# Index units ahead of the convolution units in a two-layer hybrid decoder step, with the index dots inside the convolution units

## The chip, the cores and the metric

The kernel runs on one core of one Trainium2 chip. The metric is the device time of one execution in microseconds (us). All times below are of the kernel before the change unless something else is said.

## The reference, cut to what matters

Two layers, each with one combined input projection, three parallel branches, and one output projection with a residual add. There are 528 prompt tokens (16 learned ones and 512) and 8 sample tokens; the model width is 1024.

```python
z = einsum('btd,dn->btn', rms_norm(x), w_in)            # 3624 columns
q, k, v, ga, qi, wi, ki, ub, gb, cv, cg, gc = split(z)
q = rope(rms_norm(q)); k = rope(rms_norm(k)); qi = rope(qi); ki = rope(ki)
uc = cv * sigmoid(cg)
# A: 8 index heads of 32 dims pick the keys of every query
sc = sum_h wi[h] * relu(qi[h] . ki * 32**-0.5) * 8**-0.5     # causal
idx = top_k(sc);  att = softmax attention over the picked keys
# B: causal pooling of ub.   C: depthwise convolution of width 31 over uc, LayerNorm, swish
y = concat(att * silu(ga), pool * silu(gb), conv * silu(gc)) @ w_out;  x = x + y
```

## The kernel before, in words

**Layout.** The prompt is cut into five token tiles of 16 (with the 8 sample tokens: 24 rows), 128, 128, 128 and 128 rows. The input projection is done in float32r, with the activations and the weights each split into a high part and a rest: three matmuls for every 128 rows of the contraction, so 24 for a unit. Names of engines: PE is the matmul engine, DVE the vector engine, ACT the scalar engine, POOL is GpSimd, SP issues the DMAs.

**Units.** A unit is one PSUM bank full of the projection. `unit_fm` (L1254) makes 128 channels by 268 tokens (half of them); `unit_tm` (L1236) makes one token tile by all columns of a group. The order of units (L124 to L127) is: eight convolution units `("conv", m, h)`, of which m = 0, 1 are the value channels (group cv) and m = 2, 3 the gate channels (group cg); five index units (296 columns: index queries, head weights, index key); five key units, five query units, five value units (512 columns each); then the units of `PLAN`, which lie between the 40 attention items (tile, head), and the output units. Each unit waits until the unit that had its bank before is evacuated (`open_unit`, L1215).

**Weights.** They come in pieces (`LOADS`, L69) into six slots by `m % 6`. SP loads a piece when the last unit that reads the slot is done (`w_load`, L624). ACT makes the high part (`high`, L942) and DVE the rest (`rest`, L1618); for the pieces of `REST_ON_POOL` (L84: two of q, two of v, and all from ub on) ACT scales and POOL makes the rest. `AHEAD` is the number of pieces of the first group (2 of four 128-row blocks). They are split at the very start in layer 0, and for layer 1 in step 41 and 42 of the items of layer 0 (`split_high` L377, `split_rest` L382).

**Start of layer 0.** SP issues the loads of x tiles 0 to 2, the two weight pieces, x tiles 3 and 4, constants, page table. SP then waits for the table and reads 16 page numbers (L620) before it issues anything else.

**Index.** ACT evacuates an index unit (`idx_evac`), POOL rotates it, PE transposes it (L1333), ACT keeps it in `qkT`. Then come 40 *pieces* (L141) of index scores: PE multiplies (`dots`, L1351, two pieces in a call, into bank 0 and 1 of A), ACT takes the relu in place (`relu`, L1038), DVE multiplies by the head weight and adds into `bias` (`gather`, L1671). `dots(first)` waits until DVE has gathered all earlier pieces. The 40 pieces lie in the key and query units: two behind each half of a unit.

**Keys and queries.** For every tile of k (numbers 0 to 4) and q (5 to 9): ACT copies the unit to `kz` (three buffers) and its square to `ksq` (`kq_evac`, L1014), DVE sums the squares (`kq_sum`, L1657), and POOL does all the rest in one chain (`kq_tile`, L858): power -0.5, two products over 512 columns, four operations of the rotation. POOL also makes the rests of four weight pieces between the tiles (L877). PE transposes the finished tile (`kq_turn`, L1341): tile n behind unit n+2, so that the last two (8 and 9) stand behind value units 0 and 1. `kq_evac(n)` waits for the transpose of tile n-3.

**DVE in between.** The convolution is 31 taps of two instructions each (`tap`, L1731) that accumulate in bank 2 and 3 of A: 8 taps beside the index units, 15 in the key units, 8 in the query units. Top-k is rounds of max and match_replace on `bias` (`select`, L1693); 20 of these steps lie in the query units (`between`, L1743), the others in a loop behind the query units (L1820) and in the attention items (`late`, L1719). PE's first attention scores of a tile are followed by DVE's `ttr` (L1969), which is queued behind that loop.

## Time and profile before

| what | value |
|---|---|
| time, median of 3 runs | 752.42 us (747.38, 752.42, 752.99) |
| profiled execution | 746.28 us, of which the span of the engines is 745.0 us |
| granted PE clock, mean over the span | 0.984 of full speed |
| PE (matmul) busy | 702.3 us, 94% of the span |
| DVE busy | 523.2 us, 70% |
| ACT busy | 331.2 us, 44% |
| POOL busy | 300.3 us, 40% |
| DMA | 71.90 MB, mean 97 GB/s |

The profile is of one execution. A line such as `L1260` is a line of the kernel. Matmuls overlap in their pipeline, so the busy time of PE is an upper bound of what it needs; the distance between starts is the better measure. A line `[1.20 <-DVE small L1969]` behind an instruction means that its engine was idle for 1.20 us before it and that a DVE instruction of line 1969 ended that idle time. Index dots appear as two records each, since they are float32.

### The profile page before, as it was taken

How to read it: one execution, taken by the hardware profiler on the slowest of the kernel's cores; microseconds unless marked ns; L12 is line 12 of the kernel's file. 1: busy time of each engine (PE TensorE's matmuls, PEld its weight loads, DVE VectorE, ACT ScalarE, POOL GpSimd, SP SyncE). 2: the span in 40 equal slices, each digit the busy share in tenths (PEclk: the TensorE clock that was granted, in tenths of full speed). 3: DMA queues.
4: the chain of work that ended last, by engine and by line, in shares of the span. 5: the costliest groups of instructions: out<-in, count | busy, mean ns of one | idle time of the engine just before them, and what ended most of it. 6: DMA issues, size and time to landing. Idle time of an engine off the chain costs nothing.

```text
span 745.0 us, 13366 instructions
## 1 busy us (share of the span) xinstructions
PE 702.3 (94%) x4690; PEld 567.3 (76%) x4690; DVE 523.2 (70%) x1320; ACT 331.2 (44%) x850; POOL 300.3 (40%) x445
## 2 busy tenths in 40 slices
PE   5899999999889999998999999999988799999998
PEld 5897756578777777776999866666878688777797
DVE  3538888899977977435663898989997777822232
ACT  5525646533947333334132555543485643332212
POOL 1013698942848710011120459895376763000000
PEclk9999999999989999999999999999999899999999
DMA  5543040314232536014025304031522244501203
GB/s 195 160 137 118 17 128 30 114 35 143 58 87 60 179 136 227 1 58 139 21 92 153 126 4 142 30 88 46 157 58 61 83 151 167 170 1 57 96 22 112
DMA packets 54979, 71.90 MB, mean 97 GB/s; under 512 B 12977, under 2 KB 30585, under 8 KB 54881
## 3 DMA queue, kind: packets, MB, share of 16 engines
q1 hardware_dynamic: 54802, 70.96, 30.0%
q8 instruction: 38, 0.62, 0.4%
q14 instruction: 28, 0.23, 0.1%
q10 hardware_dynamic: 111, 0.08, 0.0%
HBM read 64.05 MB, written 7.61 MB: 96 GB/s over the span
## 4 chain that ended last, share of the span: by engine, by line
PE 70%; DVE 21%; ACT 3%; issue 2%; DMA 2%; POOL 1%; SPq 0%; ACTq 0%; DVEq 0%; POOLq 0%
PE R L1273 16%; PE R L1260 6%; PE R L1244 6%; PE R L1262 6%; PE R L1261 6%; PE R L1245 6%; PE R L1246 6%; DVE bias L1715 5%; DVE small L1713 5%; PE R L1409 4%; PE A L1360 3%; PE A L1213 2%; PE A L1438 2%; DVE W_r L1614 2%; PE R L1213 1%
## 5 line engine op out<-in xcount | busy, mean ns | idle before, releaser
L1260 PE MATMUL R<-x_hi,W_r 128*128 128x268 f32 x448 | 137.7, 307 | 5.9 <-DVE bufA L1614 3.3
L1262 PE MATMUL R<-x_hi,W_r 128*128 128x268 f32 x448 | 133.3, 297 | 0.0
L1261 PE MATMUL R<-x_lo,W_r 128*128 128x268 f32 x448 | 133.0, 297 | 0.0
L1244 PE MATMUL R<-W_r,x_hi 128*128 128x512 f32 (+3 forms) x320 | 123.0, 385 | 3.3 <-DVE W_r L1614 3.3
L1273 PE MATMUL R<-yT,W 128*128 128x268 f32 (+2 forms) x768 | 124.2, 318 | 1.0 <-DVE gt L1882 1.0
L1273 PEld LDWEIGHTS R<-yT,W 128*128 128x128 f32 x768 | 106.9, 190 | 16.8 <-issue 6.2
L1245 PE MATMUL R<-W_r,x_hi 128*128 128x512 f32 (+3 forms) x320 | 118.4, 370 | 0.0
L1246 PE MATMUL R<-W_r,x_lo 128*128 128x512 f32 (+3 forms) x320 | 118.1, 369 | 0.0
L823 POOL TENSOR_TENSOR W_r<-W,W_r 128x256 fp32r<-128x256 f32 x112 | 79.4, 742 | 53.1 <-ACT W_r L940 52.3
L1260 PEld LDWEIGHTS R<-x_hi,W_r 128*128 128x128 f32 x448 | 89.5, 200 | 14.5 <-issue 8.5
L1261 PEld LDWEIGHTS R<-x_lo,W_r 128*128 128x128 f32 x448 | 89.9, 201 | 0.0
L1262 PEld LDWEIGHTS R<-x_hi,W_r 128*128 128x128 f32 x448 | 89.4, 200 | 0.0
L1134 ACT ACTIVATE pm<-zi,small 128x16 f32<-128x16 f32 x64 | 19.5, 304 | 145.2 <-PE A L1213 133.3
L1614 DVE SCALAR_TENSOR_TENSOR A<-uext,params,A 128x512 f32<-128x512 f32 x116 | 79.6, 746 | 0.0
L1244 PEld LDWEIGHTS R<-W_r,x_hi 128*128 128x128 f32 (+1 forms) x320 | 54.5, 170 | 27.8 <-DVE W_r L1614 10.2
L922 POOL TENSOR_TENSOR KV<-KV,ubx 128x256 f32<-128x256 f32 x64 | 50.6, 823 | 42.0 <-DMA KV<-in_cache_k 22.6
L1246 PEld LDWEIGHTS R<-W_r,x_lo 128*128 128x128 f32 (+1 forms) x320 | 54.5, 170 | 15.0
L1245 PEld LDWEIGHTS R<-W_r,x_hi 128*128 128x128 f32 (+1 forms) x320 | 54.7, 171 | 10.2
L1041 ACT ACTIVATE A<-A 128x264 f32<-128x264 f32 (+3 forms) x80 | 26.7, 378 | 72.3 <-PE A L1360 72.3
L1715 DVE MATCH_REPLACE8 bias<-small,bias 128x276 f32<-128x276 f32 (+3 forms) x106 | 57.9, 548 | 0.0
L1713 DVE MAX8 small<-bias 128x8 f32<-128x276 f32 (+3 forms) x106 | 56.9, 557 | 0.6
L1409 PE MATMUL R<-kT,qT 64*16 64x16 f32 (+4 forms) x160 | 37.8, 437 | 17.1 <-DVE small L1969 17.1
(259 smaller groups left out, 1219.7 us busy)
## 6 DMA issues: line engine op xcount, KB each, us to landing
W<-in_w_in SPq DMA_DIRECT2D x52, 512.0 KB, 4.7
KV<-in_cache_k SPq DMA_DIRECT2D x32, 256.0 KB, 3.0
W<-in_w_out SPq DMA_DIRECT2D x8, 1024.0 KB, 6.6
KV<-in_cache_v SPq DMA_DIRECT2D x32, 256.0 KB, 3.9
ubx<-qkv_rows SPq DMA_DIRECT2D x16, 256.0 KB, 3.5
W<-in_w_in SPq DMA_DIRECT2D x8, 296.0 KB, 3.5
out_new_k_prompt<-kz SPq DMA_DIRECT2D x8, 256.0 KB, 2.2
out_new_v_prompt<-V SPq DMA_DIRECT2D x8, 256.0 KB
```

The costliest lines, as they stand in the source:

```text
L823: done = pool.tensor_tensor(w_raw(m, W_r)[part], w_raw(m)[part], w_high(m, W_r)[part].bitcast(F32), ALU.subtract)
L1244: pe.matmul(out, x_hi[:, kc, rows], hi, start=(kc == 0), stop=False)
L1245: pe.matmul(out, x_hi[:, kc, rows], lo, start=False, stop=False)
L1246: m = pe.matmul(out, x_lo[:, kc, rows], hi, start=False, stop=(kc == KC - 1))
L1260: pe.matmul(out, hi[:, cols], x_hi[:, kc, toks], start=(kc == 0), stop=False)
L1261: pe.matmul(out, hi[:, cols], x_lo[:, kc, toks], start=False, stop=False)
L1262: m = pe.matmul(out, lo[:, cols], x_hi[:, kc, toks], start=False, stop=(kc == KC - 1))
L1273: m = pe.matmul(R[:, k, 0:hi - lo], W[:, slot(x), kc % 4, 128 * (u[1] % 4):128 * (u[1] % 4) + 128], yT[:, kc, lo:hi], start=(kc == 0), sto ...
L1409: m = pe.matmul(R[0:r, k, 0:min(w, 512)], lhs, kT[b:b + 64, h // 2, 0:min(w, 512)], start=True, stop=True)
L1614: return dve.scalar_tensor_tensor(out=out, in0=a0, scalar=s, in1=a1, op0=op0, op1=op1)
L1713: tk_s.did(dve.max(best, field))
L1715: tk_s.did(dve.match_replace(field, best, field, GONE))
```

## The change

The index group comes first in the weights and in the order of units, tiles in the order 1, 2, 0, 3, 4; then the eight convolution units. The state transposes stand ahead of the convolution units and the transposes of the index tiles behind the first three of them. All 40 index dots are in the last five convolution units, two behind every second 128-row block, in four banks of A instead of two, and a call waits for the gathers of all but the last two pieces. DVE gathers eight pieces ahead of the evacuation of each of these units and makes the weight rests 6 to 11 between them. All 31 taps are in the key units (15) and query units (16), with two `select` steps in each unit of both kinds. `AHEAD` becomes 4 pieces of two 128-row blocks (296 columns). In layer 0 all four are loaded and split at the start; for layer 1, two are split in step 41 and 42 as before, and two are loaded into the space of `V` when the last weighing of V is done, and split beside the last eight output units.

```diff
-GROUPS = [("cv", C_CV, 256, 4), ("cg", C_CV + 256, 256, 4), ("idx", C_I, 296, 2), ("k", C_K, 512, 2), ("q", C_Q, 512, 2),
+GROUPS = [("idx", C_I, 296, 2), ("cv", C_CV, 256, 4), ("cg", C_CV + 256, 256, 4), ("k", C_K, 512, 2), ("q", C_Q, 512, 2),
...
+EARLY = ([("idx", i, 0) for i in IDX_ORDER]
+         + CONV_ORDER
          + [(n, i, 0) for n in ("k", "q", "v") for i in range(NT)])
 UNITS = EARLY + [u for step in PLAN for u in step] + [("out", m, 2) for m in range(KC)]
 NUM = {u: n for n, u in enumerate(UNITS)}
...
-IX_K, IX_Q = 4, 4
+DOTS_OF = {("conv", 1, 1): 0, ("conv", 2, 0): 8, ("conv", 2, 1): 16, ("conv", 3, 0): 24, ("conv", 3, 1): 32}
...
-REST_J = (3, 7)
-TAPS_IDX, TAPS_K, TAPS_Q = 8, (3, 3, 3, 3, 3), (2, 2, 2, 1, 1)
+TAPS_K, TAPS_Q = (3, 3, 3, 3, 3), (3, 3, 3, 3, 4)
...
-            first_w(0)
-            first_w(1)
+            for m in range(AHEAD):
+                first_w(m)
...
-                eng.wait_ge(*(next_lo.at(0) if l else pre_w_lo.at(4 * m + 4)))
+                eng.wait_ge(*(next_lo.at(2 * m + j + 1 - KC) if l else pre_w_lo.at(2 * m + j + 1)))
...
                 for m in range(AHEAD, 6):
-                    if l and m < 4:
-                        sp.wait_ge(*unit_s.at(NUM["out", 3, 2] + 1 - len(UNITS)))
-                    elif l:
+                    if l:
...
-            for m in range(8, 14):
+            for m in range(8, 10):
                 w_load(m)
...
+            for m in range(10, 14):
+                w_load(m)
             def k_store(i):
...
-                for m in range(AHEAD):
+                for m in range(2):
                     next_w.did(sp.dma_start(w_raw(m), w_source(l + 1, m)))
             for n in range(16, 32):
                 kv_load(n)
+            if l + 1 < DEPTH:
+                sp.wait_ge(*PV_s.at((len(ITEMS) - HEADS) // 2))
+                sp.wait_ge(*store_s.at(store_s.n))
+                sp.wait_ge(*vm_s.at(vm_s.n))
+                sp.wait_ge(*row_v.at(16))
+                for m in range(2, AHEAD):
+                    next_w.did(sp.dma_start(w_raw(m, W, 1), w_source(l + 1, m)))
...
-            high(2)
-            if l == 0:
-                row_keep()
-            for m in range(3, 6):
-                high(m)
-            if l:
-                row_keep()
+            high(4)
+            high(5)
...
+            for i in IDX_ORDER:
+                idx_evac(i)
+            row_keep()
+            act.wait_ge(*st_t.at(1))
+            st_k.did(copy(uxs[:, :, :, 0:CONV_STATE], A[:, 0, 0:480].rearrange("p (c b j) -> p c b j", c=2, b=8)))
+            act.wait_ge(*st_t.at(2))
+            st_k.did(copy(ubs[:, :, :, 0:POOL_STATE], A[:, 1, 0:240].rearrange("p (c b j) -> p c b j", c=2, b=8)))
             high(6)
             high(7)
...
-                rel_s.did(act.activation(A[0:ROWS[i], p % 2, 0:hi - lo], A[0:ROWS[i], p % 2, 0:hi - lo], ACT.Relu,
+                rel_s.did(act.activation(A[0:ROWS[i], p % 4, 0:hi - lo], A[0:ROWS[i], p % 4, 0:hi - lo], ACT.Relu,
                                          scale=1.0 / 16))
...
+            for n in range(5):
+                for p in range(8 * n, 8 * n + 8):
+                    relu(p)
+                if n:
+                    high(7 + n)
+                if n == 3:
+                    half_tanh(0)
+            half_tanh(1)
...
-                for x in range(IX_K):
-                    relu(p)
-                    p += 1
-                    if i in (1, 2) and x == 1:
-                        scale_block(11 + i)
+                if i in (1, 2):
+                    scale_block(11 + i)
                 kq_evac(i)
...
-                    act.wait_ge(*next_w.at(16 * AHEAD))
-                    for m in range(AHEAD):
+                    act.wait_ge(*next_w.at(32))
+                    for m in range(2):
...
+            if l + 1 < DEPTH:
+                act.wait_ge(*next_w.at(16 * AHEAD))
+                for m in range(2, AHEAD):
+                    split_high(act, l + 1, m, next_hi)
...
+                        unit_s.did(m)
+                    if u in DOTS_OF and kc % 2 == 1:
+                        dots(DOTS_OF[u] + kc - 1)
...
+            def x_ready(i):
+                if l == 0:
+                    pe.wait_ge(*pre_kept.at(2 * i + 2))
+                elif i == 0:
+                    pe.wait_ge(*xd_s.at(0))
+                elif i < 3:
+                    pe.wait_ge(*res_s.at(3 * KC * i - 9 * KC))
+            def dots(first):
+                if first == 0:
+                    pe.wait_ge(*idxk_s.at(NT))
+                    pe.wait_ge(*row_s.at(3))
+                elif first >= 4:
+                    pe.wait_ge(*acc_s.at(first - 2))
+                for p in (first, first + 1):
+                    i, h, lo, hi = PIECES[p]
+                    b = 32 * (h % 4)
+                    ix_s.did(pe.matmul(A[0:ROWS[i], p % 4, 0:hi - lo], qkT[b:b + 32, h // 4, START[i]:START[i] + ROWS[i]],
+                                       qkT[b:b + 32, 2, lo:hi], start=True, stop=True))
+            def idx_turn(i):
+                n = IDX_NTH[i] - 1
+                pe.wait_ge(*idxz_s.at(n + 1))
+                if n >= 2:
+                    pe.wait_ge(*idxk_s.at(n - 1))
+                for j in range(3):
+                    m = turn(A[:, n % 2, 128 * j:128 * j + ROWS_P[i]], zi[0:ROWS_P[i], i, 128 * j:128 * j + 128], ROWS_P[i])
+                idxt_s.did(m)
+            for i in IDX_ORDER:
+                x_ready(i)
+                if l == 0 and i == 0:
+                    pe.wait_ge(*pre_par_k.at(DEPTH))
+                unit_tm(("idx", i, 0), "idx")
+                if l == 0 and i == 1:
+                    first_params(pe)
+                    first_turn(pe, 3)
+                    first_turn(pe, 4)
+                if l and i == 2:
+                    pe.wait_ge(*sa_s.at(0))
+                    for x in range(NT):
+                        m = pe.matmul(A[0:SR, 3, x:x + 1], row[:, XCOL[x]:XCOL[x] + SR], ones[:, 0:1], start=True, stop=True)
+                    stats_s.did(m)
...
             pe.wait_ge(*diag_s.at(NT))
             if l == 0:
                 pe.wait_ge(*pre_ones.at(2))
             spread(diag, row_t)
...
-            for i in range(NT):
-                unit_tm(("idx", i, 0), "idx")
...
-            pe.wait_ge(*st_k.at(2))
-            for i in range(NT):
...
+            pe.wait_ge(*state_s.at(48))
...
+            turns_behind = {("conv", 0, 0): (1, 2), ("conv", 1, 0): (0, 3), ("conv", 0, 1): (4,)}
+            for u in CONV_ORDER:
+                unit_fm(u, ("cv", "cg")[u[1] // 2], 128 * (u[1] % 2))
+                if u == ("conv", 0, 0):
+                    pe.wait_ge(*st_k.at(2))
+                for i in turns_behind.get(u, ()):
+                    idx_turn(i)
...
                 pe.wait_ge(*kz_s.at(n + 1))
                 if n >= 2:
                     pe.wait_ge(*kqk_s.at(n - 1))
+                else:
+                    wait_evac(pe, ("conv", 3, 1))
...
-                rest(2)
-                rest(3)
-                rest(4)
-                rest(5)
...
-            if l == 0:
-                rest(2)
-                rest(3)
+            rest(4)
+            rest(5)
...
                 dst = area(i, SENT + lo, SENT + hi)
                 w = zi[0:ROWS[i], i, 384 + h:385 + h]
-                src = A[0:ROWS[i], p % 2, 0:hi - lo]
...
-            p = 0
             for u in CONV_ORDER:
+                if u in DOTS_OF:
+                    for p in range(DOTS_OF[u], DOTS_OF[u] + 8):
...
-                        rest(x)
+                if u in (("conv", 0, 0), ("conv", 1, 0)):
+                    rest(6 + m)
+                if m >= 2:
+                    rest(8 + 2 * (m - 2) + h)
             conv_in(0)
...
-            for j in range(TAPS_IDX):
-                tap(j)
-                if j == REST_J[0]:
-                    rest(8)
-                    rest(9)
-                if j == REST_J[1]:
-                    rest(10)
-                    rest(11)
-            j = TAPS_IDX
+            j = 0
             for i in range(NT):
...
-                    p += 2
-                    for _ in range(TAPS_K[i] // 2 if x else (TAPS_K[i] + 1) // 2):
-                        tap(j)
-                        j += 1
+                for x in range(TAPS_K[i]):
+                    tap(j)
+                    j += 1
+                between(2)
                 kq_sum(i)
             rest(14)
             rest(15)
             for i in range(NT):
-                for x in range(0, IX_Q, 2):
-                    gather(p)
-                    gather(p + 1)
-                    p += 2
-                    for _ in range(TAPS_Q[i] // 2 if x else (TAPS_Q[i] + 1) // 2):
-                        tap(j)
-                        j += 1
-                    if x:
-                        kq_sum(NT + i)
-                    between(2)
+                for x in range(TAPS_Q[i]):
+                    tap(j)
+                    j += 1
+                kq_sum(NT + i)
+                between(2)
             rest(18)
             rest(19)
-            assert j == CONV_W and p == len(PIECES) and acc_s.n == ACC_END
+            assert j == CONV_W and acc_s.n == ACC_END
             dve.wait_ge(*st_k.at(2))
...
                 take(("out", m, 2))
+                if l + 1 < DEPTH and m < 4:
+                    dve.wait_ge(*next_hi.at(m + 5))
+                    split_rest(dve, l + 1, 2 + m // 2, m % 2, next_lo)
```

## Rows read from the trace of the kernel before

**Rows 1.** Windows of layer 0, all engines, busy us: ahead of the key units, and key and query units

```profile
core 0: us, PE busy (x) PEld busy (x) DVE busy (x) ACT busy (x) POOL busy (x), PEclk, DMA share, GB/s
13.00:68.00 55.00, 50.65 (x366) 48.60 (x367) 32.05 (x70) 26.98 (x66) 9.19 (x26) 0.97 0.41 128
68.00:152.00 84.00, 82.09 (x382) 51.09 (x381) 73.89 (x147) 45.01 (x94) 67.28 (x90) 1.00 0.24 73
```

**Rows 2.** Waits of POOL from 78 to 157 us: in total, times, longest

```profile
POOL small L863 <- DVE small L1663: 12.7, 3, 11.2
```

**Rows 3.** Timeline of POOL: start, duration, instruction

```profile
78.72 0.23 POOL L863 TENSOR_SCALAR small<-small 24x8 f32<-24x8 f32 x1 [11.24 <-DVE small L1663]
...
91.72 2.82 POOL L823 TENSOR_TENSOR W_r<-W,W_r 128x256 fp32r<-128x256 f32 x4
...
156.09 0.46 POOL L872 TENSOR_TENSOR kz<-rot_tmp 128x128 f32<-128x128 f32 x1
...
435.75 0.23 POOL L863 TENSOR_SCALAR small<-small 24x8 f32<-24x8 f32 x1 [11.22 <-DVE small L1663]
```

**Rows 4.** Timeline of PE, from the first key unit to the attention items

```profile
67.84 0.47 PE L1244 MATMUL R<-W_r,x_hi 128*24 128x512 f32 x1
...
99.52 0.94 PE L1360 MATMUL A<-qkT 32*128 32x400 f32 x4
100.39 0.50 PE L1244 MATMUL R<-W_r,x_hi 128*128 128x512 f32 x1
...
157.69 0.48 PE L1244 MATMUL R<-W_r,x_hi 128*128 128x512 f32 x1
...
177.12 0.22 PE L1409 MATMUL R<-kT,qT 64*16 64x16 f32 x4
```

**Rows 5.** Groups of PE by line, 68 to 152 us: busy, mean ns, idle

```profile
L1244 PE MATMUL R<-W_r,x_hi 128*128 128x512 f32 (+1 forms) x89 | 37.1, 417 | 1.7 <-DVE W_r L1614 1.7
...
L1360 PE MATMUL A<-qkT 32*128 32x264 f32 (+3 forms) x80 | 14.4, 437 | 0.3 <-DVE bias L1614 0.3
```

**Rows 6.** Groups of DVE by line and form, whole span

```profile
L1614 DVE SCALAR_TENSOR_TENSOR A<-uext,params,A 128x512 f32<-128x512 f32 x116 | 79.6, 746 | 0.0
...
L1614 DVE SCALAR_TENSOR_TENSOR W_r<-W,params,W_r 128x512 fp32r<-128x512 f32 x32 | 23.6, 798 | 4.0 <-ACT W_r L940 4.0
...
L1614 DVE SCALAR_TENSOR_TENSOR bias<-A,zi,bias 128x264 f32<-128x264 f32 x28 | 13.7, 490 | 5.2 <-ACT A L1041 3.5
```

**Rows 7.** Timelines of SP, ACT and PE at the start of layer 0

```profile
25.47 2.15 SPq L638 DMA_DIRECT2D W<-in_w_in  x4
...
29.29 1.71 ACT L940 ACTIVATE W_r<-W,params 128x256 fp32r<-128x256 f32 x4 [5.34 <-DMA W<-in_w_in]
...
34.66 0.39 PE L1260 MATMUL R<-x_hi,W_r 128*128 128x268 f32 x1 [3.28 <-DVE bufA L1614]
...
35.01 0.29 PE L1262 MATMUL R<-x_hi,W_r 128*128 128x268 f32 x1
35.14 0.28 PE L1260 MATMUL R<-x_hi,W_r 128*128 128x268 f32 x1
...
38.35 0.43 PE L1260 MATMUL R<-x_hi,W_r 128*128 128x268 f32 x1
```

**Rows 8.** Waits of PE, 177 to 200 us, and DVE's first item

```profile
PE R L1409 <- DVE small L1969: 2.2, 2, 1.2
PE R L1468 <- DVE ubs L1849: 0.6, 1, 0.6
...
180.92 0.15 DVE L1969 CUSTOM_DVE_ANT_0 zi<-R,cst 16x16 f32<-16x16 f32 x1
```

**Rows 9.** Timeline of PE and ACT at the end of layer 0

```profile
346.90 3.29 ACT L380 ACTIVATE W_r<-W,params 128x256 fp32r<-128x256 f32 x8
...
350.60 1.16 PE L1448 MATMUL A<-pmT,Vm 128*128 128x128 f32 x8 [1.19 <-ACT pmT L940]
...
354.15 3.87 PE L1273 MATMUL R<-yT,W 128*128 128x132 f32 x32 [0.96 <-DVE gt L1882]
```

More of the change, by code:

```diff
@@ L1061, in scalar_layer @@
             for i in range(NT):
-                for x in range(IX_Q):
-                    relu(p)
-                    p += 1
-                    if i in (1, 2) and x == 1:
-                        scale_block(15 + i)
+                if i in (1, 2):
+                    scale_block(15 + i)
                 kq_evac(NT + i)
@@ L1250, in unit_tm @@
                         unit_s.did(m)
-                    if first_dots is not None and kc % 4 == 3:
-                        dots(first_dots + kc // 4 * 2)
             def unit_fm(u, name, col):
```

161 lines of the change are left out of this document (52 added, 109 removed).

## The prediction

> **What bounds the kernel now.** I read the stage windows first. From 68 to 152 us, the key and query units, PE is busy for 82.1 of 84 us, DVE for 73.9 and POOL for 67.3 [rows 1]: three engines are near their limit at once, so the busy shares don't say which of them sets the time. The waits do. Over 78 to 157 us POOL waited only three times, 12.7 us, of which 11.2 us is the wait for its first key tile; so 1.5 us in the 77.8 us behind that [rows 2]. Its chain of ten key and query tiles and four weight rests begins at 78.72 and ends at 156.55 (156.09 + 0.46) [rows 3]. Value unit 2 stands behind the transpose of the last tile and begins at 157.69, 1.1 us behind that end [rows 4]. PE waited for no more than 1.7 + 0.3 us in this stretch [rows 5]. So PE and POOL are in balance: each arrives when the other does. Ahead of the key units (13 to 68 us) DVE is busy for only 32 of 55 us [rows 1]; that is the room the change wants to use. Behind the value units the attention items are paced by DVE: PE waits 2.2 + 0.6 us for it up to 200 us [rows 8]. Layer 1 repeats all of this 357.0 us later (POOL's first tile at 435.75 against 78.72 [rows 3]).
>
> **The change part by part.** I follow three moments in each layer: the start K of the first key unit (67.84 now), the start T of POOL's first tile (78.72), and the start V of value unit 2 (157.69) [rows 3, 4].
>
> *Dots moved.* All 40 index dots (two passes each, 80 records) leave the key and query units and stand ahead of K. They are busy for 14.4 us [rows 5]. By start distances a pair of 400 columns takes 0.87 us (99.52 to 100.39) [rows 4], and the shorter ones less; I take 13 us for the 20 calls (between 10 and 14.4). PE's sum doesn't change, but K comes 13 us later.
>
> *Pace of the dots.* In the five units with dots PE needs 5 x 24 matmuls at 0.125 us (35.01 to 35.14 at the higher clock) [rows 7], 15 us, and 13 us of dots, 28 us. DVE has in the same time 40 gathers of about 0.5 us [rows 6] with some extra instructions for head 0, 22 us; five evacuations, 2 us; and four weight rests of two pieces at 0.75 us, 6 us: 30 us. They overlap, with two pairs of slack from the four banks. I add 1.5 us for waits; the bounds are 0 (PE alone) and 6 (each handover at a unit's edge seen in full).
>
> *Start of layer 0.* Now PE waits 3.28 us for row factors and weights at 34.66 [rows 7]. This wait goes, but another comes: index unit 4 needs the bank of the first index unit, whose evacuation is queued on ACT behind the high parts of pieces 4 and 5. Their loads leave SP only after the page numbers, at 25.47, and the first such piece was ready for ACT at 29.29 [rows 7]. SP has two more issues and 0.16 MB more ahead of the table, which I take as 0.8 us. So: 29.29 + 0.8, two high parts of 1.71 us, 0.8 for the evacuation: 34.4 to 35. PE, beginning 0.6 us earlier with pieces of 303 instead of 524 KB, has done four index units and the turns at about 30.5. A wait of some 4.5 us replaces 3.3: +1.5 (0 to 4), with the start -0.6.
>
> *Index turns behind convolution units.* They waited for POOL and ACT for some tenths of a microsecond; the convolution units hide them now: -0.8. Of what moved past them, the loads of pieces 6 to 9 wait for index unit 4 on SP and the page loads stand behind them; they are needed 15 us later and cost nothing unless SP falls behind by that much. K is then at 67.8 + 13 + 1.5 + 1.5 - 0.6 - 0.8 = 82.4 in layer 0 (+14.6) and +13.7 in layer 1.
>
> *From K to T.* Now it is 10.9 us (78.72 less 67.84): a unit with dots in it and a DVE with taps in front of the sum. Then it will be: DVE's last gathers and evacuation 1.4 behind K, a rest of 1.5, the two convolution inputs 1.5, three taps of two instructions (0.67 apart by their starts, 0.746 long [rows 6]) 4.1, two selects 0.5, the sum 0.7: 9.7 us. So T moves by 13.4 and 12.5 us.
>
> *From T to V.* POOL's chain has no instruction less. Without its two short waits it takes 77.8 - 1.5 = 76.3 us. PE for itself needs, from K to V, the 89.85 us of now (67.84 to 157.69) less 13 of dots and 2 of waits: 74.8. It could be at V at 157.2; POOL ends at 92.1 + 76.3 = 168.4, and V is at 169.5. Now PE waits for POOL, in front of the transposes of the query tiles: kz has three buffers, the units are in program order, and no value unit can go ahead. V moves by 13.4 - 1.5 = +11.9 in layer 0 and +11.0 in layer 1. The taps cost nothing here: DVE has 62 tap instructions at 0.67, 41.5 us, ten sums, twenty selects and two weight rests, together about 60 us, beside a chain of 76; with that cover gone, the 8 added taps are 11 us.
>
> *Behind V.* Three value units and the first scores follow V unchanged: scores at 177.12 + 11.9 = 189.0. DVE's first item stands at 180.92 now, behind its top-k loop [rows 8]. The last sum of squares comes some 4.7 us later than now, so the loop ends at about 185.6, before PE arrives. The 2.8 us for which PE waited for DVE up to 200 us [rows 8] are then taken up. Left: +9.1 in layer 0 and, with 2.7, +8.3 in layer 1 (if DVE takes up nothing: 11.9 and 11.0).
>
> *Two more pieces ahead for layer 1.* ACT's block at 346.90 goes from 8 x 256 columns, 3.29 us, to 4 x 296, some 2.0; DVE's likewise, and it begins with the first piece. PE's waits of 1.19 and 0.96 us behind them go [rows 9]: -2.2. The other two pieces are split beside the last output units, where DVE waits for PE; that cover gone, four rests of half a microsecond would cost 2 us. If their load comes late, the squares on ACT behind it hold DVE and so PE; the load leaves at about 350 and is wanted at 359, where a piece now is ready 3.8 us behind its issue [rows 7].
>
> **Sum.** +9.1 + 8.3 - 2.2 = +15.2 us. On the profiled execution that is 746.3 + 15.2 = 761.5 us. The median of the runs shown is 6.1 us above the profiled one; on it the sum is 767.6. I take the middle, 765 us.
>
> **The rivals.**
>
> A. *POOL keeps up, and the kernel is faster.* If POOL's tiles could run at PE's pace, V would be at 157.2 and 156.3 (-0.4 and -1.3), and with the -2.2 at the layer's edge the sum is -3.9: 742.4 on the profiled execution, 748.5 on the median, 745.5 in the middle. It decides at the point where K + 9.7 + POOL's chain and the 1.1 us behind it are under K + 74.8, so for a chain under 64 us. For it: PE is busy for 82.1 of 84 us [rows 1], which reads as if it alone were the limit. Against it: the chain is 76.3 us with a wait of 1.5 only [rows 2, 3].
>
> B. *The clock falls behind PE's new waits.* Behind the wait of 3.28 us at 34.66 a matmul of 268 columns grew from 0.28 to 0.43 us, the lower of the two levels (1.2 for 2.4 GHz), and was so until 38.35 at least, 3.7 us behind the restart [rows 7]. The new waits in the query units (one for each weight rest of POOL, 2.8 us [rows 3], and then 4 to 5 us ahead of value units 0 and 1) are as long. If the value units behind run at the lower level, 24 matmuls of 512 columns take 24 x (512/1.2 - 512/2.4) ns = 5.1 us more; in one or two units of each layer that is +13 together, 778 us. Against it: most such units stand ahead of another wait for POOL, which swallows the loss. The Trainium skill bears on this: its page "TensorE: Matmul & The Clock Gate", section "HAM oscillation — how this bites in real kernels", says that an engine that idles between tiles falls back to the lower clock again for every tile. By it each of these waits would be paid for, and the time be that of B.
>
> C. *Only half of the shift survives.* DVE's and ACT's slack in the items absorbs more than 2.8 us, or T comes earlier since PE passes the conv stage at DVE's cost: +7, 757 us. For it: DVE is idle for 20 us of the query stage. Against it: its order is fixed, and the items of layer 0 lie behind the same scores.
>
> D. *The change doesn't do what it says* (the dots' unit doesn't hide DVE's gathers, but adds to them): this is the 6 us bound of the pace above, and lies inside the range.
>
> **How the numbers follow.** Forecast 0.66, A 0.14, B 0.10, C 0.10. About 1% (7.5 us) is what a measurement of this kernel can tell from no change; so slower means over 759.9, faster under 744.9. Half of A is faster: 0.07. Same: the other half of A, half of C, and 0.04 of the forecast's lower end: 0.16. Slower: 0.77. The forecast's own bounds are +5 to +25 around its middle 765 (dots 10 to 14.4, pace 0 to 6 and start 0 to 4, DVE taking up 0 to 5); with C and most of B the range is 753 to 779, which leaves out A and the far end of B.
>
> **What would show it.** Right: POOL's first tile at 90 to 94 us with chains of 76 us behind it, hardly a wait inside; PE's waits for POOL (`kz`) of 10 us or more in each layer, where now there are none; value unit 2 near 169; DVE busy for less in the query units. K at 81 to 84. PE waiting for less at 350. Wrong: if PE shows no waits in the query units and K to V is 75 us, A holds. If the granted clock in the value units is under 1, B. If V is late but the first item is not, C.

## The result, and the profile after the change

The changed kernel takes 774.57 us (median of 4 runs, 773.06 to 776.36), against 751.46 us (747.38 to 752.99) for the kernel before: 1.032 times as long, 95% interval 1.027 to 1.037. The forecast was 765 us. The profiled execution took 773.06 us, its span 771.7 us: +26.7 us on the span of before, where the sum of the prediction was +15.2. On the medians it is +23.1: the profile of before (746.3 us, mean granted clock 0.984) is one of the fastest executions of that kernel, so the stages below show 3.6 us more than the medians do.

The three moments of the prediction first: K (first key unit), T (POOL's first tile), V (value unit 2), then the first scores and DVE's first item, all of layer 0, and K, T and the first scores of layer 1. They answer to [rows 3], [rows 4] and [rows 8]. Columns: start, duration, instruction, and in brackets the idle time before it and what ended it.

```profile
83.33 0.41 PE L1256 MATMUL R<-W_r,x_hi 128*24 128x512 f32 x1
...
93.30 0.24 POOL L885 TENSOR_SCALAR small<-small 24x8 f32<-24x8 f32 x1 [52.27 <-DVE small L1671]
...
169.62 0.46 POOL L894 TENSOR_TENSOR kz<-rot_tmp 128x128 f32<-128x128 f32 x1
...
170.54 0.48 PE L1256 MATMUL R<-W_r,x_hi 128*128 128x512 f32 x1
...
189.97 0.19 PE L1422 MATMUL R<-kT,qT 64*16 64x16 f32 x2
...
190.37 0.16 DVE L1963 CUSTOM_DVE_ANT_0 zi<-R,cst 16x16 f32<-16x16 f32 x1 [2.03 <-PE R L1422]
...
455.16 0.41 PE L1256 MATMUL R<-W_r,x_hi 128*24 128x512 f32 x1
...
465.11 0.24 POOL L885 TENSOR_SCALAR small<-small 24x8 f32<-24x8 f32 x1 [51.33 <-DVE small L1671]
...
562.04 0.22 PE L1422 MATMUL R<-kT,qT 64*16 64x16 f32 x4
```

K moved by 15.5 us, T by 14.6, the first scores by 12.9. POOL's chain fills the whole distance from T to V: it ends at 169.62 + 0.46 = 170.08, and V stands 0.5 us behind. The roles at the first item have changed: before, PE came at 177.12 and DVE at 180.92; now DVE has been idle for 2.03 us when PE's scores come.

The waits of the whole run, in total, times and longest:

```profile
POOL small L885 <- DVE small L1671: 103.6, 2, 52.3
...
PE R L1422 <- DVE small L1963: 13.9, 10, 2.5
PE R L1227 <- POOL kz L894: 13.0, 7, 3.1
PE R L1256 <- POOL W_r L845: 6.2, 4, 2.5
```

POOL waits for the first tile of each layer and for no other one, and PE now waits for POOL: 19.2 us in the two layers. In these units PE waits for POOL by 6.4 us for tiles and 3.6 us for weight rests in layer 0. Before, it had 1.7 + 0.3 us of waits there, none of them for a tile [rows 5]. The windows of layer 0 (up to K, K to V, V to the first scores) show the same: PE is busy for 76.9 of 87 us beside POOL.

```profile
13.00:83.00 70.00, 66.22 (x442) 54.85 (x443) 37.92 (x91) 38.80 (x104) 7.89 (x26) 0.98 0.35 102
83.00:170.00 87.00, 76.94 (x328) 51.57 (x324) 79.03 (x160) 33.15 (x55) 71.65 (x96) 0.94 0.22 69
170.00:190.00 20.00, 20.00 (x159) 16.14 (x160) 18.09 (x51) 9.42 (x20) 5.75 (x9) 1.00 0.28 85
```

Stage by stage, by the starts in the two traces (each stage ends where the next begins):

| stage | forecast | measured |
|---|---|---|
| up to K, layer 0 | +14.6 | +15.5 |
| K to first scores (109.3 before) | -2.7 | -2.6 |
| first to last scores (158.7) | -2.8 | +1.4 |
| last scores to the last eight output units (24.6) | -2.2 | -2.4 |
| from there to K of layer 1 (64.4) | +13.7 | +18.4 |
| K to first scores, layer 1 (109.3) | -2.7 | -2.4 |
| first to last scores, layer 1 (161.7) | -2.7 | -2.9 |
| to the end (49.2) | 0 | +1.7 |
| sum | +15.2 | +26.7 |

### The profile page after: what moved, and what is told of

It is laid out like the page before. It is cut to its first block, busy times and chain, and to the rows that moved or that the text cites. A ratio compares the mean times of both kernels' runs of the same rounds, so it can differ in the third digit from the quotient of the medians.

```text
span 771.7 us, 13377 instructions
## 1 busy us (share of the span) xinstructions
PE 721.3 (93%) x4690; PEld 580.1 (75%) x4690; DVE 533.8 (69%) x1320; ACT 332.2 (43%) x850; POOL 302.1 (39%) x445
## 4 chain that ended last, share of the span: by engine, by line
PE 67%; POOL 15%; DVE 10%; issue 3%; ACT 3%; DMA 2%; SPq 0%; POOLq 0%; DVEq 0%; ACTq 0%
PE R L1286 16%; PE R L1270 7%; PE R L1271 5%; PE R L1272 5%; PE R L1256 5%; PE R L1257 5%; PE R L1258 5%; PE R L1422 4%; POOL W_r L845 3%; POOL small L887 3%; PE A L1317 3%; PE A L1227 3%; POOL kz L891 3%; PE A L1451 2%; POOL kz L889 2%
## 5 line engine op out<-in xcount | busy, mean ns | idle before, releaser
L1270 PE MATMUL R<-x_hi,W_r 128*128 128x268 f32 x448 | 141.6, 316 | 0.9 <-issue 0.9
L1272 PE MATMUL R<-x_hi,W_r 128*128 128x268 f32 x448 | 132.4, 296 | 0.0
L1256 PE MATMUL R<-W_r,x_hi 128*128 128x512 f32 (+3 forms) x300 | 120.0, 400 | 11.0 <-POOL W_r L845 6.2
L1286 PE MATMUL R<-yT,W 128*128 128x268 f32 (+2 forms) x768 | 127.5, 324 | 0.0
L1286 PEld LDWEIGHTS R<-yT,W 128*128 128x128 f32 x768 | 110.2, 196 | 15.8 <-issue 7.1
L1257 PE MATMUL R<-W_r,x_hi 128*128 128x512 f32 (+3 forms) x300 | 117.8, 393 | 0.0
L845 POOL TENSOR_TENSOR W_r<-W,W_r 128x256 fp32r<-128x256 f32 x112 | 85.2, 792 | 44.8 <-ACT W_r L962 44.0
L1627 DVE SCALAR_TENSOR_TENSOR A<-uext,params,A 128x512 f32<-128x512 f32 x116 | 77.9, 741 | 0.0
L1256 PEld LDWEIGHTS R<-W_r,x_hi 128*128 128x128 f32 (+1 forms) x300 | 53.4, 178 | 30.6 <-POOL W_r L845 9.4
L944 POOL TENSOR_TENSOR KV<-KV,ubx 128x256 f32<-128x256 f32 x64 | 51.1, 829 | 45.6 <-issue 24.6
L1258 PEld LDWEIGHTS R<-W_r,x_lo 128*128 128x128 f32 (+1 forms) x300 | 53.6, 179 | 16.8 <-issue 4.3
L1257 PEld LDWEIGHTS R<-W_r,x_hi 128*128 128x128 f32 (+1 forms) x300 | 53.7, 179 | 14.6 <-issue 3.2
L953 POOL TENSOR_TENSOR row<-row,bufB 128x268 f32<-128x268 f32 (+2 forms) x21 | 11.9, 568 | 104.8 <-ACT bufB L1123 104.8
```

The source lines that it names most:

```text
L845: done = pool.tensor_tensor(w_raw(m, W_r)[part], w_raw(m)[part], w_high(m, W_r)[part].bitcast(F32), ALU.subtract)
L1256: pe.matmul(out, x_hi[:, kc, rows], hi, start=(kc == 0), stop=False)
L1257: pe.matmul(out, x_hi[:, kc, rows], lo, start=False, stop=False)
L1258: m = pe.matmul(out, x_lo[:, kc, rows], hi, start=False, stop=(kc == KC - 1))
L1270: pe.matmul(out, hi[:, cols], x_hi[:, kc, toks], start=(kc == 0), stop=False)
L1272: m = pe.matmul(out, lo[:, cols], x_hi[:, kc, toks], start=False, stop=(kc == KC - 1))
```

## The experiments

Twelve more kernels ran. "After" is the changed kernel, 774.6 us. Each run stands beside runs of the kernel before, so I give its ratio to that one with the 95% interval. The milestones of layer 0 (and K and the first scores of layer 1), from the timelines of the profiled runs:

| kernel | K | T | chain ends | first scores | first item | K, layer 1 | first scores | median us |
|---|---|---|---|---|---|---|---|---|
| before | 67.8 | 78.7 | 156.6 | 177.1 | 180.9 | 424.9 | 534.1 | 751.5 |
| after | 83.3 | 93.3 | 170.1 | 190.0 | 190.4 | 455.2 | 562.0 | 774.6 |
| e1, after, gamma short | 83.6 | 93.6 | 159.6 | 180.1 | 183.4 | 445.4 | 541.8 | 753.5 |
| e2, before, gamma short | 67.2 | 78.1 | 152.2 | 176.5 | 180.4 | 430.6 | 539.9 | 752.1 |
| e3, rests on DVE | 85.0 | 95.0 | 163.0 | 185.8 | 188.0 | 450.1 | 551.0 | 759.9 |
| e4, first sum early | 84.1 | 92.3 | 169.8 | 189.7 | 190.1 | 454.5 | 562.4 | 772.2 |
| e5, dots narrow | 84.6 | 94.6 | 171.2 | 191.1 | 191.5 | 456.6 | 563.2 | 772.4 |
| e6, 8 taps short | 82.1 | 92.1 | 168.9 | 188.8 | 189.2 | 455.0 | 561.7 | 774.8 |
| e7, evacuate first | 77.8 | 87.8 | 164.8 | 184.7 | 185.1 | 450.8 | 557.5 | 769.1 |
| e8, half the dots back | 73.2 | 85.6 | 163.0 | 184.3 | 184.7 | 441.0 | 552.1 | 763.1 |
| e9, e3 + e7 and more | 79.0 | 89.0 | 157.3 | 177.7 | 182.2 | 445.1 | 545.1 | 756.5 |
| e10, gathers short | 81.2 | 90.7 | 167.6 | 187.5 | 187.9 | 451.8 | 558.1 | 771.9 |
| e11, e8 + e7 and more | 67.5 | 79.9 | 153.7 | 175.4 | 178.6 | 430.6 | 538.1 | 749.2 |
| e12, before, more POOL | 68.4 | 79.2 | 166.2 | 186.4 | 186.8 | 432.4 | 551.1 | 766.2 |

### Is POOL's chain the bound? (e1, e2, e12, e6, e4)

**e1 and e2** shorten one product of POOL, in the kernel after and in the kernel before: it is made for one head of eight and left out for the others.

```diff
-kzg_s.did(pool.tensor_tensor(z, z, gam[0:r, w, :].unsqueeze(1).broadcast_to([r, HEADS, HD]), ALU.mult))
+kzg_s.did(pool.tensor_tensor(z[:, 0:1, :], z[:, 0:1, :], gam[0:r, w, :].unsqueeze(1).broadcast_to([r, 1, HD]), ALU.mult))
```

> The kernel after, with POOL's gamma product of every key and query tile made for one head of eight (the product for the other seven is left out). Theory (POOL's chain from T to V sets the pace): the product took 1.28 us, so each tile loses about 1.0 and the chain of 77.2 us about 10. PE needs 74.8 us from K to V by itself and has 87.2, so V moves from 170.5 to about 160.5, PE's waits for POOL (13.0 + 6.2 us in the whole run) fall to about 2, and the first item comes at about 182 (DVE's loop now ends at 188.3 with 7.2 us of idle in it, so not before 181). In all about -8.5 us a layer: 757 us (753 to 762). Rival 1 (PE's own work or DVE sets the pace in the key and query units, and the waits for POOL only stand where another wait would): 771 to 775. Rival 2 (clock): the dips in the items stay where they are, so only the waits' length changes.

> The kernel before, with the same product for one head of eight. Theory (PE and POOL in balance before the change): PE has only 2 us of waits from K to V there, so V can move by 1 to 2 us, and the first item, which waits for DVE, by less: 748 to 752, no change that can be measured. Rival (POOL was the bound before the change too, and PE's waits were hidden in its queue): about -10 us a layer, 732 us.

e1 took 753.5 us, ratio 1.003 (1.000 to 1.006); e2 752.1 us, ratio 0.999 (0.996 to 1.002). The same edit is worth 21 us in the kernel after and nothing in the kernel before. The chain became 10.8 us shorter (65.97 for 76.78), the first scores came 9.8 us earlier in layer 0 and 20.2 in layer 1. In e2, from K to the first scores it is 109.25 us, in the kernel before 109.28. So POOL sets the time after the change; before it, POOL held nothing that could be had back. PE's waits for POOL in e1:

```profile
PE R L1227 <- POOL kz L894: 5.0, 4, 1.5
```

**e12** lengthens POOL's chain in the kernel before, by making one sum three times.

```diff
+for _ in range(2):
+    kzg_s.did(pool.tensor_tensor(z[:, :, 0:16], ta, tb, ALU.add))
+    pool.wait_ge(*kzg_s.at(kzg_s.n))
 kz_s.did(pool.tensor_tensor(z[:, :, 0:16], ta, tb, ALU.add))
```

> The kernel before, with the last sum of the rotation (128 columns, 0.46 us, some 0.54 with its gap) made three times instead of once in each of the ten tiles: 10.8 us more for POOL a layer. Theory (PE and POOL in balance before the change, 1.5 us of slack in POOL's chain): V and the first scores come 9.3 us later in each layer, the first items 5.5 to 7 us, PE waits for POOL by 8 us or more a layer where it had no such waits: 765 us (761 to 769). Rival (POOL was off the path before the change): 752 to 754.

It took 766.2 us, ratio 1.020 (1.015 to 1.026), and the first scores moved by 9.24 us where 9.3 was expected; counted from K, which itself stood 0.5 us later, it is 8.7 us, and 9.4 in layer 1. So the kernel before has hardly more slack on POOL than its 1.5 us of waits. Waits for a tile appear in PE (with those for POOL's rests 6.6 us in layer 0, less than the 8 I expected):

```profile
PE R L1216 <- POOL kz L875: 11.0, 4, 4.5
```

and DVE is now the one that waits at the first item, as in the kernel after:

```profile
186.76 0.16 DVE L1972 CUSTOM_DVE_ANT_0 zi<-R,cst 16x16 f32<-16x16 f32 x1 [3.80 <-PE R L1412]
```

**e6** takes 16 of DVE's tap operations in the query units down to 16 columns.

```diff
 src, so_far = uext[:, c, N_META + j:NTOK + j], A[:, 2 + c, :]
+if j in (16, 17, 19, 20, 22, 23, 25, 26):
+    src, so_far = src[:, 0:16], so_far[:, 0:16]
```

> The kernel after, with 8 of the 15 or 16 taps in the query units made on 16 of 512 columns (the convolution leaves those taps out): 16 operations of DVE from 0.74 to about 0.1 us, 10 us less work for DVE. Theory (the taps lie beside POOL's chain and cost nothing; behind V the first item waits for PE): V stays at 170.5 within 1 us, the first item at 190.4 within 1, time 772 to 775. If POOL's rests, which took 4.47 us instead of 2.83 beside DVE's own, change with it, V may come 1 to 2 us earlier. Rival (DVE holds the key and query units): -8 to -10 us a layer, 757 us.

774.8 us, ratio 1.031 (1.029 to 1.034): nothing. From K to the first scores it is 106.70 us, after the change 106.64. The taps cost nothing beside POOL's chain, as the prediction said.

**e4** makes the first sum earlier: `if i == 0 and x == 1: kq_sum(0)` within the taps, instead of behind them and `between(2)`.

> The kernel after, with the sum of the first key tile made behind the second tap instead of behind three taps and two top-k steps. Theory (the chain begins with that sum and has no slack behind it): the sum moves from 92.46 to about 90.6, T from 93.3 to 91.3, and V by the same 2.0 us, in both layers; the first item by as much or a little less: -3.5 us, 771 us (769 to 773). Rival (the pace is PE's or DVE's): T moves and V doesn't, 774 to 775.

772.2 us, ratio 1.027 (1.021 to 1.033). K to T fell by 1.8 us (9.97 to 8.16), K to the first scores by 1.1 in layer 0 and not at all in layer 1 (+1.0). In layer 0 the chain behind T took 0.7 us longer (77.5 for 76.8). In layer 1 the chain did end 2.3 us earlier (539.84 for 542.14), but the value unit behind it ran at the lower clock: its first matmul has a duration of 0.78 us (0.48 at V above), and the unit takes 8.25 us instead of 5.8.

```profile
533.72 1.12 PE L1227 MATMUL R<-cst,kz 128*128 128x128 f32 x4 [2.73 <-POOL kz L894]
534.48 0.78 PE L1256 MATMUL R<-W_r,x_hi 128*128 128x512 f32 x1
```

I had expected V to come 2.0 us earlier in both layers. So an earlier T is worth at most what it moves, and rival B's mechanism can take it back. That is one profile; whether it always falls there isn't settled.

### What does the stage with the dots cost? (e5, e10)

**e5** makes every dot for 16 columns, **e10** every gather but those of head 0.

```diff
-ix_s.did(pe.matmul(A[0:ROWS[i], p % 4, 0:hi - lo], qkT[b:b + 32, h // 4, START[i]:START[i] + ROWS[i]],
-                   qkT[b:b + 32, 2, lo:hi], start=True, stop=True))
+ix_s.did(pe.matmul(A[0:ROWS[i], p % 4, 0:16], qkT[b:b + 32, h // 4, START[i]:START[i] + ROWS[i]],
+                   qkT[b:b + 32, 2, lo:lo + 16], start=True, stop=True))
```

```diff
 src = A[0:ROWS[i], p % 4, 0:hi - lo]
+if h:
+    src, dst = src[:, 0:16], dst[:, 0:16]
```

> The kernel after, with every index dot made for 16 columns of 144 to 400 (the other scores are left out; ReLU and gathers keep their size). The stage with the dots takes 32.9 us in either layer: 16.05 of weight matmuls, 13.0 of dots, 0.9 of waits, and some 2.6 us by which the six matmuls between two calls take longer (0.94 for 0.80 us). Theory (PE's 33 us and DVE's some 30 us of gathers, evacuations and weight rests are nearly the same, so DVE becomes the bound): the stage falls to about 30 us, K comes 3 us earlier, PE shows waits for DVE's gathers of 6 us or more a layer, and the time is 768 us (765 to 771). Rival (DVE has plenty of room in the stage): K comes 8 to 10 us earlier, 757 us.

> The kernel after, with every gather but those of head 0 made on 16 columns (the scores of the other heads are left out); PE's dots are whole again. With short dots the stage was no shorter; in its first part PE gained 1.9 us over eight calls and then waited 1.2 us for a gather, and behind that PE ran at the lower clock. Theory (PE's own 32 us and DVE's lie within 1 or 2 us of each other in the stage): now PE alone sets it, 32.0 us instead of 32.9, T is 1 to 2 us earlier, 771 us (769 to 774). Rival (DVE sets the pace of the stage and PE's matmuls only look longer): the stage falls to 29 us, 767 us.

e5 took 772.4 us (ratio 1.027, 1.024 to 1.029) and e10 771.9 us (1.026, 1.021 to 1.032). The stage (the five convolution units with dots, up to K) is 32.8 us long after the change in both layers. With short gathers it is 31.7 us without any wait: that is PE's own time, and DVE adds 1.1 us. With short dots it is 33.5 and 31.8 us, and K isn't earlier. But e5 doesn't show DVE's pace cleanly, since the clock fell in it in layer 0. Windows of e5, layer 0 (columns as in [rows 1]; the last but two is the granted clock):

```profile
51.00:65.00 14.00, 13.71 (x109) 11.74 (x107) 9.99 (x25) 7.59 (x23) 0.00 (x0) 1.00 0.51 153
65.00:85.00 20.00, 19.07 (x95) 16.37 (x96) 14.48 (x29) 9.70 (x25) 0.00 (x0) 0.57 0.09 27
```

PE waited once, for 1.2 us, was busy for 19.07 of 20 us, and yet ran near half its clock. So e5 bounds DVE's pace only from one side; e10 is the clean one. My expectation for e5 (waits for gathers of 6 us a layer, 765 to 771 us) was wrong: the waits are 1.2 and 2.0 us.

Why PE's own 31.7 and not the forecast's 28? After the change, the six matmuls between two calls (start, duration):

```profile
51.45 0.52 PE L1317 MATMUL A<-qkT 32*128 32x144 f32 x4
51.90 0.39 PE L1270 MATMUL R<-x_hi,W_r 128*128 128x268 f32 x1
52.13 0.29 PE L1271 MATMUL R<-x_lo,W_r 128*128 128x268 f32 x1
...
52.50 0.29 PE L1271 MATMUL R<-x_lo,W_r 128*128 128x268 f32 x1
52.63 0.28 PE L1272 MATMUL R<-x_hi,W_r 128*128 128x268 f32 x1
52.84 0.50 PE L1317 MATMUL A<-qkT 32*128 32x272 f32 x2
```

Between matmuls of one kind the starts are 0.12 to 0.13 us apart; behind the dots it is 0.23, and ahead of the next dots 0.21. So six matmuls take 0.94 us instead of 0.75. In e10, where PE never waits in this stage, the 120 weight matmuls take 18.7 us by their starts instead of 15.0: 3.7 us for the 20 calls, nearly 0.19 us for each. The dots themselves (0.45 us in this call, 13.0 in all) were sized rightly. 13.0 + 15.0 + 3.7 = 31.7.

The kernel before paid the same price in its key and query units. Around the call of [rows 4]:

```profile
98.95 0.40 PE L1245 MATMUL R<-W_r,x_hi 128*128 128x512 f32 x1
99.19 0.40 PE L1246 MATMUL R<-W_r,x_lo 128*128 128x512 f32 x1
...
100.72 0.40 PE L1245 MATMUL R<-W_r,x_hi 128*128 128x512 f32 x1
100.96 0.39 PE L1246 MATMUL R<-W_r,x_lo 128*128 128x512 f32 x1
```

Here matmuls of one kind start 0.23 to 0.24 us apart, but it is 0.33 us from the last one to the dots (99.19 to 99.52) and 0.33 from the first one behind them to the next (100.39 to 100.72): 0.19 us again. So this call's price is not the 0.87 us from its start to the next matmul but 1.06, and the switch costs the same on either side of the move.

### The start of layer 0 (e7)

```diff
-high(4)
-high(5)
 act.wait_ge(*rinv_s.at(1))
...
 for i in IDX_ORDER:
     idx_evac(i)
+    if i == IDX_ORDER[0]:
+        high(4)
+        high(5)
```

> The kernel after, with ACT evacuating the first index unit ahead of the high parts of pieces 4 and 5 instead of behind them. Theory (the wait of 2.88 us at 33.04 is for that evacuation): the wait goes, index unit 4 starts at 30.2, the lower clock behind the wait (1.7 us of longer matmuls) goes too, and everything behind is 3 to 4.5 us earlier in layer 0, nothing in layer 1: 771 us (770 to 772). Rival (the wait only moves: the convolution units then wait for pieces 4 and 5): 774.

769.1 us, ratio 1.023 (1.020 to 1.026): -5.4 us, K at 77.78. The wait that goes, in the kernel after:

```profile
33.04 0.37 PE L1256 MATMUL R<-W_r,x_hi 128*128 128x296 f32 x1 [2.88 <-issue]
```

It is named "issue", that is, no releaser was found; that it goes when the evacuation is moved shows what it was for. With it went 1.7 us of longer matmuls at the lower clock. The rest of the 5.55 us at K isn't the edit's: the second index unit, which stands ahead of it, began at 19.39 for 20.23. Single profiles differ by as much: e1, e3, e4 and e6 change nothing ahead of K, and their K lies between 82.09 and 85.01. So the edit is worth 4.6 us on the trace, at the upper end of the 3 to 4.5 expected; the median is below its range (770 to 772).

### Half the dots back, and who can take POOL's work (e8, e3, e9, e11)

**e8** puts 20 of the 40 dots back behind the halves of the key units, into two banks; `DOTS_OF` keeps four for each convolution unit.

```diff
-DOTS_OF = {("conv", 1, 1): 0, ("conv", 2, 0): 8, ("conv", 2, 1): 16, ("conv", 3, 0): 24, ("conv", 3, 1): 32}
+DOTS_OF = {("conv", 1, 1): 0, ("conv", 2, 0): 4, ("conv", 2, 1): 8, ("conv", 3, 0): 12, ("conv", 3, 1): 16}
...
-unit_tm(("k", i, 0), "k")
+unit_tm(("k", i, 0), "k", 20 + 4 * i)
```

> The kernel after, with half of the index dots put back: 20 in the last five convolution units (two calls in each) and 20 in the key units (two calls in each), as before the change. Theory (what counts is how early POOL's chain starts, since PE has 12 us of waits beside it): K moves by half of the 16 us that the dots cost, to 75.5, T to about 86, V to 163 (-7.5 us); DVE's loop ends no earlier than 181 since only its idle time of 7 us can be saved. In all -7 us a layer: 760 us (756 to 765). Rival 1 (DVE with gathers and taps in the key units falls behind, so the sums come late): V -3, 768 us. Rival 2 (where the dots stand makes no difference): 774 us.

763.1 us, ratio 1.016 (1.012 to 1.020). K came 10.1 us earlier (8 expected), T 7.7, the chain's length stayed 77.4 us, and the first scores came 5.7 us earlier. Undoing half of the move gives back half of the loss (11.5 of 23.1 us on the medians).

**e3** gives the rests of pieces 12, 13, 16 and 17 to DVE; ACT no longer scales these pieces for POOL.

```diff
-REST_ON_POOL = [FIRST[G["q"]], FIRST[G["q"]] + 1, FIRST[G["v"]], FIRST[G["v"]] + 1] + list(
+REST_ON_POOL = list(
...
 kq_sum(i)
+if i in (2, 3):
+    rest(10 + i)
```

> The kernel after, with the rests of the four pieces 12, 13, 16 and 17 made by DVE instead of POOL, all work done. Theory (POOL's chain sets V, DVE's loop sets the first item as soon as V is early): the chain loses 4 rests of 2.83 us (two of them stretched to 4.47 and 4.14), so V comes at PE's own pace, about 158 to 160 instead of 170.5. DVE gets 8 operations of 0.75 us, 6 us, and loses 7.2 us of idle: its loop ends at 187 instead of 188.3, the first item at 187.5 instead of 190.4, and PE waits for DVE in the first items for 6 to 8 us instead of 2.7. In all -3 us a layer: 768 us (764 to 772). Rival (only V counts, DVE catches up within the items): -10 us a layer, 753 us.

759.9 us, ratio 1.011 (1.005 to 1.017), between my value and the rival's and below my range (764 to 772). The first item came at 187.95 (187.5 expected), in part by luck, since K stood 1.7 us late in this profile. V didn't come at PE's pace (POOL's chain ended at 163.0, V was expected at 158 to 160): PE now waits for DVE's rests of pieces 14, 15 and 18, 19, which stand behind the sums.

```profile
PE R L1249 <- DVE W_r L1620: 9.3, 4, 3.0
...
PE R L1220 <- POOL kz L894: 3.8, 7, 0.8
```

**e9** adds the edit of e7, and moves two top-k steps (one `between(2)`) behind each of these two pairs of rests. **e11** is e8 with the edit of e7, the rests of 16 and 17 on DVE and one such move.

> The kernel after with three edits, all work done: the rests of pieces 12, 13, 16 and 17 on DVE (as in the run that gave 759.9), the first index unit evacuated ahead of pieces 4 and 5 (as in the run that gave 769.1, -5.5), and two top-k steps moved behind the rests of pieces 14, 15 and 18, 19, for which PE had waited 1.66 and 2.98 us. If these add up: 760 - 5.5 - 1 to 3 = 752 us (749 to 755), level with the kernel before. Rival (DVE's whole work up to the first item is the bound of each layer, 103 us behind K, so that its order doesn't matter): 754.5.

> The kernel after with half of the dots back in the key units (the run that gave 763.1), the first index unit evacuated first (-5.5), the rests of pieces 16 and 17 on DVE and two top-k steps behind the rests of 18 and 19; all work done. K comes at 67.7 as before the change, POOL's chain is 77.4 - 5.7 us, DVE's work from K to the first item 109 + 3 us, so the first item comes at about 179.5 (180.9 in the kernel before); in layer 1 the convolution stage is 6.7 us longer than before the change and gives back 1.5: 754 us (750 to 758). Rival (POOL's relief doesn't show, since DVE is behind the first item now): 757.5.

e9 took 756.5 us, ratio 1.007 (1.004 to 1.010): slower than the 749 to 755 expected, nearer to its rival (754.5). In e3 and e9 alike the first item stands 103 us behind K (102.94, 103.17), whatever the order, and DVE is busy for 101.9 and 102.2 us of it: DVE's own work is the bound there. e11 took 749.2 us (750 to 758 expected), ratio 0.998 (0.996 to 1.001): level with the kernel before, the best version with the new order of units, and no gain over the old one that can be measured.

## Why the prediction was right, and where its size was off

**Right: the bound.** "Now PE waits for POOL": T at 93.3 (92.1 forecast), chain 76.8 us (76.3), V at 170.5 (169.5), first scores at 190.0 (189.0). PE's waits for POOL from K to V are 10.0 us in layer 0, the least of what was named. e1, e2 and e12 show that it is the cause and not a coincidence of lengths, and e8 that the loss goes with the start of the chain. *Two more pieces ahead*: -2.4 for -2.2; the two waits at the layer's edge are gone, but no run tried this part alone.

**Mis-sized: "Pace of the dots".** Forecast 28 us + 1.5; measured 32.8 in each layer. The dots were right (13.0), DVE's delays too (1.1 for 1.5); the term left out is the switch between dots and weight matmuls, 3.7 us a layer. I had taken 0.125 us for every matmul from an uninterrupted unit, and for the dots the 0.87 us from their start to the next matmul, although the wider distances on both sides of them stand in the same stretch of the kernel before. The 6 us of rival D cover the size, but by another cause: D had DVE's gathers in mind.

**Off in the other direction: "Start of layer 0".** +1.5 forecast; the new wait was 2.88 instead of 4.5 us, since the first such piece was ready for ACT at 28.95 and not at 30.1; index unit 4 began at 33.04 (34.4 to 35 forecast, with the same two high parts and evacuation in between). That is most of the reason why the +3.3 of dots appear at K of layer 0 as +0.9 only; with K differing by 2.9 us between profiles (e7), no finer account of it can be given. e7 shows the wait's whole price, 4.6 us with the clock: I had counted its length alone.

**Failed: "DVE takes up 2.8 behind V", as a term of the total.** The taking up is there at first (the first scores stand 12.85 us later than before, the fourth group 10.38 us: 205.38 for 195.00), but from first to last scores layer 0 took 1.4 us more. These two stretches before, and the same two after the change (layer 0, layer 1; columns as in [rows 1]):

```profile
177.12:335.84 158.72, 148.57 (x1023) 123.13 (x1023) 115.53 (x316) 76.42 (x227) 60.90 (x77) 0.98 0.33 104
534.13:695.79 161.66, 151.21 (x1023) 126.02 (x1023) 107.95 (x301) 74.01 (x220) 55.96 (x72) 0.96 0.30 95
189.97:350.14 160.17, 152.09 (x1023) 126.78 (x1023) 115.65 (x307) 76.20 (x227) 60.82 (x77) 0.95 0.32 101
562.04:720.78 158.74, 150.99 (x1024) 125.48 (x1024) 108.66 (x291) 74.11 (x220) 56.48 (x72) 0.96 0.31 98
```

In layer 0 PE's idle time fell by 2.1 us (158.72 - 148.57 = 10.15 to 8.08), but the same 1023 instructions kept it busy for 3.5 us longer, at a granted clock of 0.95 for 0.98. In layer 1, with 0.96 both times, the busy time stayed and the idle time fell by 2.7. One of the slow places is the unit at 216.83, with matmuls of 0.43 us for 0.28; another is

```profile
272.00:282.00 10.00, 8.23 (x41) 6.67 (x41) 6.80 (x21) 2.67 (x9) 2.79 (x4) 0.66 0.77 268
```

So of the 4.2 us by which this row missed, the clock has 3.5. But the fall in idle time isn't safe either. Over the 14 profiles (28 such stretches) PE's busy time follows the clock, from 148.2 us at 0.98 to 153.8 at 0.94, while its idle time lies anywhere between 7.7 and 12.3 us. The whole distance is between 157.1 and 164.5 us; on the mean it is 160.9 where DVE was waiting for the first scores (16 stretches) and 161.3 where PE's scores came first (12). These are stretches of different kernels, so the means are rough; but of the 2.8 us no more than 0.4 is left on them, so the -2.9 of layer 1, which looks like a hit, is in part luck. Where DVE's lead goes within the items stays open.

Two other parts of the missing 11.5 us are the clock's: +1.6 in the last output units of layer 0 (in the row of +18.4) and +1.7 in those of layer 1, where the clock fell below full in the kernel after and not in the kernel before. Together 6.8 us (3.5 + 1.6 + 1.7) belong to the clock, 0.7 us to idle time that was not taken up, and 4 us to the dots' stage, less what the start gave. That the clock is lower *because* of the change isn't shown: no run isolates it.

**Rival A** (POOL keeps up) fell, but e1 comes near its case: with POOL faster, the loss is gone (753.5 us). The prediction of it, faster than before (742 to 748), was too good. The reason is a balance that I hadn't drawn up: from the first unit of layer 1 to its K it is 62.75 us for 46.0, so the dots' stage costs 16.8 us, and between K and the first item e1 gains 13.4 us (113.1 us before, 99.7 in e1, in both layers), with DVE busy for 95.2 us of the 99.7. By these numbers the move loses 3.4 us a layer even with e1's short chain. e1's chain of 66.0 us is still above the 64 of A's condition, and PE still waits for POOL in it, so A itself wasn't reached.

**Rival B** (the clock) came in part. Value unit 0 did run at the lower level behind its wait of 2.88 us (matmuls of 0.63 us from 153.94 on, 0.40 behind V), and the loss was swallowed by the next wait for POOL, as argued against B; e4's layer 1 shows the other outcome. Elsewhere the clock cost the 6.8 us above. The Trainium skill's page "TensorE: Matmul & The Clock Gate", section "HAM oscillation — how this bites in real kernels", says that a kernel that waits ahead of every tile starts every tile at the lower clock. Here some waits were paid for and some weren't: the one of 2.48 us that ends at 273.77 after the change lies in the stretch at 0.66 above, while the one of 2.70 us that ends at 261.93 in the kernel before is followed by 10 us at 1.00. And some dips had hardly a gap ahead of them (below).

**Rival C** (half of the shift survives) fell: the first item stands 9.45 us later than before in layer 0, and DVE was ahead of PE there, so it had nothing more to give.

## What to carry to other kernels

Two engines that arrive together are both the bound: before taking work from the one that is busy for 98% of a stage, look for the chain of another that fills the same distance with no waits, and ask what starts that chain. Work that is moved ahead of the chain's start costs its full time, and the room it leaves behind is worth nothing until the chain is shorter. And price a small operation between large ones by the distance between the starts of its neighbours on both sides, less what they need without it: 99.19 to 100.72, less twice 0.235, is 1.06 us for a call whose own distance to the next matmul is 0.87.

## What the runs showed of the hardware that was not expected

**The lower clock on a busy engine.** In e5 PE ran at 0.57 of its clock on the mean of 20 us, while it was busy for 19.07 of them; what the edit had changed was the width of its dots, 16 columns. The only wait near is the 1.22 us up to 65.93, and the same places of the kernel after the change have waits of 0.36 and 0.53 us and a clock of 1.00. All four runs of e5 have a lower mean clock (0.942 to 0.953) than the four after the change (0.958 to 0.971). After the change, the first 5 us of the last output units show 0.73 with PE busy throughout and no wait in front; the kernel before had waited there for 1.19 and 0.96 us [rows 9] and kept its clock.

```profile
370.00:375.00 5.00, 5.00 (x43) 4.96 (x43) 2.17 (x6) 0.31 (x1) 0.46 (x1) 0.73 0.25 77
```

**Weight rests of DVE and POOL at the same time slow each other.** POOL's four operations of a rest take 2.82 us in the kernel before [rows 3]. In the kernel after, two of four such rests a layer fall beside DVE's own rests:

```profile
105.68 2.83 POOL L845 TENSOR_TENSOR W_r<-W,W_r 128x256 fp32r<-128x256 f32 x4
...
114.77 4.47 POOL L845 TENSOR_TENSOR W_r<-W,W_r 128x256 fp32r<-128x256 f32 x4
```

```profile
114.19 4.46 DVE L1627 SCALAR_TENSOR_TENSOR W_r<-W,params,W_r 128x512 fp32r<-128x512 f32 x4
```

DVE's four would take about 2.8 us (a pair is 1.41). Both together last 5.05 us, from 114.19 to 119.24; one after the other they would be 5.6. The Trainium skill's page "SBUF — State Buffer", section "Who interferes with whom", says that a DVE instruction with two SBUF inputs contends with a GpSimd instruction that reads SBUF, and that the pair of ports they share is an exclusive lock. The trace agrees nearly: the two series are only 0.6 us shorter together than one after the other. It cost POOL's chain 3.0 us in layer 0 (its 16 operations are busy for 14.3 us in all, 11.3 before) and 2.5 in layer 1. In layer 0 the chain was still only 0.5 us longer than forecast (76.8 for 76.3), since POOL's rotations ran faster than before (each of the two of 64 columns 0.32 us for 0.43 on the mean), which I hadn't foreseen either.
